# Two edits on TensorE's list: first block-attention scores without the wait on the value tiles' evictions, the sparse gates' token layout behind the next projection

## The reference, cut to what matters

```python
# first block: block attention (moba), stick-breaking attention, latent attention
proj = hn @ w_in
qa, ka, va = ...                       # 8 heads of 64
y_a = moba_attention(partial_rope(qa), partial_rope(ka), va)
# second block: sparse attention with three branches, a gate for each head and branch
proj = h @ w_in[l]
q_a, kv_a, g_a, q_b, k_b, v_b, uv_c = jnp.split(proj, IN_OFFSETS, axis=-1)
o_a = nsa_attention(..., jax.nn.sigmoid(g_a).reshape(B, S, NSA_HEADS, 3), ...)
kc = compress(k_cmp, ...)              # gelu(blocks @ w1) @ w2, the same for the values
out = gb[..., 0:1] * o_cmp + gb[..., 1:2] * o_slc + gb[..., 2:3] * o_win
```

## Time and profile before

| what | value |
|---|---|
| median of 3 runs | 2306.53 us (2305.97 to 2306.60) |
| the profiled execution, its own time | 2306.26 us |
| its span, first to last instruction | 2304.6 us |
| around the span | 1.7 us |
| PE busy | 2242.3 us, 97% |
| DVE, ACT, POOL busy | 71%, 54%, 3% |
| transfers | 467 MB, 203 GB/s on average |
| share of PE in the chain that ended last | 88% |

### The profile page before, as it was taken

One profiled execution on the slowest core, in us unless ns is written; L12 is line 12 of the kernel. 1 busy time (PEld: TensorE's weight loads), 2 busy tenths in 40 slices (PEclk: granted clock), 3 DMA queues, 4 the chain that ended last, 5 costly groups with the idle time before them and its releaser, 6 DMA issues.

```text
span 2304.6 us, 38375 instructions
## 1 busy us (share of the span) xinstructions
PE 2242.3 (97%) x14760; PEld 2007.8 (87%) x14760; DVE 1632.8 (71%) x2331; ACT 1234.9 (54%) x1729; POOL 75.0 (3%) x143
## 2 busy tenths in 40 slices
PE   3999999999999999999999999999999999999999
PEld 2888999988888888999988889899888898898888
DVE  7888777678778887677685667666756676667655
ACT  4444567564446446585554465656544555565443
POOL 0100000000000100000000000000000000000000
PEclk9999999999999999999999999999999999999999
DMA  8887465547666875655555546334555463344552
GB/s 321 298 290 270 166 226 178 199 159 282 253 239 218 284 282 187 221 189 215 192 202 198 182 160 207 147 128 166 195 186 183 150 240 140 137 165 176 190 187 104
DMA packets 79509, 467.32 MB, mean 203 GB/s; under 512 B 10080, under 2 KB 10800, under 8 KB 33168
## 3 DMA queue, kind: packets, MB, share of 16 engines
q1 hardware_dynamic: 58480, 389.12, 47.2%
q0 software_dynamic: 19312, 71.74, 8.8%
q10 hardware_dynamic: 1584, 4.62, 0.5%
HBM read 458.56 MB, written 1.05 MB: 199 GB/s over the span
## 4 chain that ended last, share of the span: by engine, by line
PE 88%; ACT 4%; DVE 4%; issue 1%; DMA 1%; ACTq 1%; DVEq 1%
PE ps L811 21%; PE ps L526 17%; PE ps L528 16%; PE ps L527 16%; PE ps L813 10%; DVE wlo L1716 2%; PE ps L640 2%; DMA adat<-in_ada 1%; PE ps L654 1%; PE ps L687 1%; ACT merged L1270 1%; DVE hx L1820 1%; ACT whi L1156 1%; PE ps L606 0%; PE ps L596 0%
## 5 line engine op out<-in xcount | busy, mean ns | idle before, releaser
L1716 DVE TENSOR_TENSOR wlo<-raw,whi 128x2048 fp32r<-128x2048 f32 x360 | 823.7, 2291 | 208.9 <-ACT whi L1156 195.2
L1156 ACT ACTIVATE whi<-raw 128x2048 fp32r<-128x2048 f32 x359 | 686.2, 1913 | 223.5 <-PE ps L528 219.4
L811 PE MATMUL ps<-hx,whi 128*128 128x512 f32 x2112 | 749.8, 399 | 5.3 <-DVE hx L1820 3.7
L813 PE MATMUL ps<-hx,wlo 128*128 128x256 f32 x2112 | 593.4, 281 | 0.0
L811 PEld LDWEIGHTS ps<-hx,whi 128*128 128x128 f32 x2112 | 397.7, 188 | 105.2 <-issue 4.7
L526 PE MATMUL ps<-hx,whi 128*128 128x256 f32 (+1 forms) x1424 | 410.8, 288 | 1.1 <-DVE wlo L1716 1.1
L527 PE MATMUL ps<-hx,whi 128*128 128x256 f32 (+1 forms) x1424 | 402.6, 283 | 0.0
L528 PE MATMUL ps<-hx,wlo 128*128 128x256 f32 (+1 forms) x1424 | 402.6, 283 | 0.0
L813 PEld LDWEIGHTS ps<-hx,wlo 128*128 128x128 f32 x2112 | 399.7, 189 | 2.1
L526 PEld LDWEIGHTS ps<-hx,whi 128*128 128x128 f32 (+1 forms) x1424 | 272.1, 191 | 7.8 <-issue 4.8
L527 PEld LDWEIGHTS ps<-hx,whi 128*128 128x128 f32 (+1 forms) x1424 | 272.4, 191 | 0.2
(11 more groups left out here) (276 smaller groups left out, 2944.5 us busy)
## 6 DMA issues: line engine op xcount, KB each, us to landing
raw<-in_w SPq DMA_DIRECT2D x360, 1024.0 KB, 4.9
adat<-in_ada POOLq DMA_DIRECT2D x128, 512.0 KB, 4.7
raw<-in_ada SPq DMA_DIRECT2D x4, 512.0 KB, 8.3
blk<-in_block POOLq DMA_DIRECT2D x2, 926.5 KB, 5.4
set_a<-set_b SPq DMA_DIRECT2D x24, 64.0 KB
x<-in_x POOLq DMA_DIRECT2D x1, 1024.0 KB, 10.2
raw<-in_ada ACTq DMA_DIRECT2D x2, 512.0 KB, 14.3
set_b<-in_ada SPq DMA_DIRECT2D x2, 512.0 KB, 12.6
```

The costliest lines, as they stand in the source:

```text
L811: mm(ps[:, bank + i, :].rearrange("p (a s) -> p a s", a=2), whi[:, slot, col:col + P], hx[:, :, k, :], start=(k == 0), stop=False)
L813: last = mm(ps[:, bank + i, 0:S], wlo[:, slot, col:col + P], hhi[:, k, :], start=False, stop=(k == KD - 1))
L1156: A(whi[:, slot, :], raw[:, slot, :], ACT.Copy).then_inc(*T.counts("hi_ready"))
L1716: tt(wlo[:, slot, :], raw[:, slot, :], whi[:, slot, :].bitcast(F32), ALU.subtract)\
```

## The change

Two edits on PE's list; the lists of the other engines stay as they are, except that all line numbers behind the first edit are lower by one. The first takes away a wait for the last eviction (the second value tile) ahead of the first scores, and leaves the wait for the ropes. The second moves the two transposes of the gates behind the 48 matmuls of tile 6. The wait for the gates' eviction (`pj_out`), which stood ahead of the transposes, stays where it was, now ahead of tile 6.

```diff
                     project("tokens")
                     project("tokens")
-                    pe.wait_ge(*T.nth("pj_out", T.n["fills"]))
                     wait_ropes(4)
...
                     pe.wait_ge(*T.nth("pj_out", T.n["fills"]))

                     def gates_by_token():
                         for t in range(2):
                             last = mm(ps[:, 6, t * 32:t * 32 + 24], gT[0:24, t * P:(t + 1) * P],
                                       c("ident", 24)[:, 0:24], start=True, stop=True)
                         return last

+                    project("features")
                     aux(gates_by_token)
-                    project("features")
                     for kind in range(2):
                         pe.wait_ge(*T.next("xb_ready"))
```

## The result

The changed kernel takes 2311.62 us (median of 13 executions, 2310.79 to 2313.11) against 2306.53: 5.1 us more, a ratio of 1.0023 with a 95% interval of 1.0015 to 1.0031. The interval is clear of 1, so the kernel is slower. Of the 13 executions of the kernel before, one took 5648.3 us, for which nothing here gives a reason; the other 12 lie between 2305.27 and 2306.99.

What follows compares the result with a forecast made beforehand. The prediction took PE's own list plus its waits as the bound (PE busy 97% of the span). From 2306.53 us, -1.5 for the first edit and +6.7 for the second gave 2311.6 us, range 2308.5 to 2314.8.

Steps and rivals of the forecast that it cites:

- The sum: Whole kernel: -1.5 us from the first edit and +6.7 from the second, +5.2 in all, said as 2311.6 us.
- First edit: First scores in each of two layers: starting 0.21 us behind the projection's last matmul, 0.76 earlier, 1.5 us saved in all.
- Second edit, PE alone: PE at the gates' transposes: worth nothing, the 0.46 us wait stays, now ahead of tile 6.
- Second edit, ACT: ACT's in-order list: the gates' copy starts at 1402.69 instead of 1396.76, and the split of tile 8 waits with it.
- The stalls: PE waits for late `wlo` at tile 8 (1.6 us) and tile 9 (1.4 us); 3.3 us a layer, 6.7 in two.
- The margin: Tile 8's weights, ready at 1402.38 and now wanted at 1405.51, may be 3.1 us later; the copy moves by 5.9.
- free: Rival, chance 0.06: moved transposes cost nothing, tile 8's weights still come in time, only the first edit counts; 2305.0 us.
- No third stall: Tile 11: weights ready 1.5 us in time, so no further PE wait; the rival third stall, 2314.4 us, had chance 0.06.
- The clock: Rival, chance 0.07: PE's clock falls behind the stalls, 2.1 us lost once in each layer; 2315.8 us.
- only one stall: Rival, chance 0.05: DVE's split of tile 9 comes in time, so a layer costs 1.9 us; 2308.8 us.
- the first edit gives nothing: Rival, chance 0.03: another wait takes over at the first scores or the gain is lost later; 2313.1 us.

Runs made afterwards that it cites:

- E1: First edit alone on the kernel before: no wait for the last value tile's eviction ahead of the first scores; 2304.65 us against 2306.10.
- E4: Changed kernel with ACT's gates copy behind the split of tile 8 and PE's wait for the gates' eviction directly ahead of the transposes; 2303.77 us against 2306.10 before.
- E6: Changed kernel with only PE's wait for the gates' eviction moved from ahead of tile 6 to directly ahead of the transposes; 2310.26 us against 2306.66 before.
- E7: Changed kernel with the gates' transposes in the middle of tile 6, behind 24 of its 48 matmuls; 2305.83 us against 2306.37 before.
- E5: Changed kernel with DVE's second key rope behind the splits of tiles 9 and 10, first differential-attention rope two splits later; 2308.70 us against 2306.66 before.
- E3: Changed kernel with ACT's copy of the transposed gates moved behind the split of tile 8 and tile 6's eviction; 2305.11 us against 2306.10 before.

## Why the prediction was right, point by point

**The sum.** Forecast 2311.6, measured 2311.62 and 2311.45. The terms were -1.5 and +6.7; alone they measured -1.45 and +7.13. That the medians agree to 0.02 is luck: the 13 executions spread over 2.3 us, and 2311.6 was chosen between 2311.4 and 2311.7. What the traces bear out is each term to 0.1 us a layer. The prediction gave 0.67 to a slowdown beyond its bound of 2311.1; the median lies 0.5 above it, but the interval of the ratio reaches to both sides of it, so this part stays undecided.

**First edit.** Right in place and size. The scores stand 0.21 us behind the projection, the ropes' wait did not take over, E1 has the 1.5 us, and between the two layers' scores the traces have the 0.76 (E1 above: 0.8).

**Second edit, PE alone.** Right: the 0.46 us in front of L995 came back in front of tile 6, 0.9 in both layers as before. E4 and E6 show what the wait costs once it is moved as well: 1.3 to 1.5 us, where I had 1.2.

**Second edit, ACT.** Right: from tile 6's start at 1395.91 the copy came after 6.60, forecast 6.58 (1402.69 - 1396.11).

**The stalls.** Right. I counted them from start to start, 1.6 and 1.4. The rows say 1.40 and 1.31, since they count from the modelled end of the last matmul, 0.28 behind its start where the next could have followed after 0.12. From start to start the first is 1406.90 - (1402.40 + 0.10 + 2.82) = 1.58, the second 1411.35 - (1406.90 + 0.10 + 2.88) = 1.47. The second is 0.1 above the forecast: PE began 0.15 behind the split's end (1411.20), not 0.05, as in E7 (0.15 again). Tile 11 came 21.86 us behind tile 6's start (1417.77 - 1395.91), where it had been 18.47 behind L995's (1414.58 - 1396.11): 3.39 for the first layer against 3.33 forecast. The second layer has 1893.88 - 1872.04 = 21.84 against 1887.29 - 1868.82 = 18.47, 3.37.

**The margin.** Right in what followed from it, wrong in what it compared. The rival of the free transposes sets tile 8's 3.1 us against the 5.9 by which the copy moves. But `wlo` of tile 8 moves by less, by its own times 1404.74 - 1400.09 = 4.65, measured 4.67 from tile 6's start: that is 1.6 over the 3.1, the first stall. And the tile that runs late first is tile 9, at a hold-up of some 2.8 us (E7). Both tiles were over their limits, so the conclusion stands.

**No third stall.** Right. The split of tile 11 on ACT waited 1.23 us for its load, which landed 1411.68 - 1406.85 = 4.8 us after `wlo` of tile 8 was done; `wlo` was ready at 1413.63 + 2.29 = 1415.92, 1.8 us in time.

**The clock.** It did not fall. The matmuls behind the stalls keep their pace of 0.12: from tile 9 at 1411.35 to tile 11 at 1417.77 are 6.42 us with the first matmul's 0.1, against 6.37. The granted clock agrees. In the stretch of the stalls (columns: PE, PEld, DVE, ACT, POOL busy, then granted clock, DMA share, GB/s):

```profile
1401.00:1415.00 14.00, 11.29 (x91) 10.74 (x90) 10.05 (x7) 9.68 (x8) 0.00 (x0) 1.00 0.43 163
```

PE was busy for 11.29 of 14 us, and the clock stayed at 1.00, the level of 2.4 GHz. Alone this column would be weak evidence, and so is the earlier trace rows in the prediction. Early in the kernel, where the matmuls of 128x512 follow at 0.64 in both profiles, it reads 0.50 after the change and 1.00 before it:

```profile
44.00:48.00 4.00, 4.00 (x13) 3.42 (x14) 3.40 (x10) 4.00 (x9) 0.15 (x1) 0.50 0.99 414
44.00:48.00 4.00, 4.00 (x13) 3.42 (x14) 3.41 (x10) 4.00 (x9) 0.20 (x1) 1.00 0.99 417
```

So the column can miss a slow stretch, and the pace decides. The Trainium skill (TensorE: Matmul & The Clock Gate, Part 1: The HAM clock gate) says that the clock falls once PE has been idle for long enough. The trace doesn't contradict it: two stalls of 1.40 and 1.31 us with tile 8's matmuls between them brought no fall.

The other rivals: *free* fell by the four new waits, *only one stall* by the second of them in each layer, *the first edit gives nothing* by E1, and E5 shows what one stall comes to: 2308.7, for which the prediction had 2308.8.

## What to carry to other kernels

When an instruction is moved on one engine, look at the list of the engine that waits for it: what is queued behind that waiting instruction moves too. Here a copy of 0.21 us took the next weight tile's conversion along, and 5.95 us of delay cost 3.4 us a layer, of which 3.05 are stalls; half the delay cost 0.28 of stalls; and with the copy moved as well there were none. Follow the delay through to each later tile: the slack of the first tile (here 4.4 us) says nothing of the next one's (2.8). And a wait has to move with the instructions that need it, or the edit frees nothing.

## What was not expected

The slow first matmuls last differently long from one execution to the next. Before, the pace of 0.64 us ends between 47.89 and 48.50; in the profile after, with the same instructions on PE up to there, it lasted 1.3 us longer (start us, us):

```profile
49.12 0.63 PE L811 MATMUL ps<-hx,whi 128*128 128x512 f32 x1
49.76 0.47 PE L811 MATMUL ps<-hx,whi 128*128 128x512 f32 x1
50.19 0.40 PE L811 MATMUL ps<-hx,whi 128*128 128x512 f32 x1
```

This is time at 1.2 GHz ahead of the rise: the granted clock there reads 0.50 (the rows above). At 0.64 against 0.35 from one such matmul to the next, 1.3 us more of it lose 1.3 x (1 - 0.35 / 0.64) = 0.6 us. The first scores came at 275.78 where the prediction has 274.98, 0.8 late, before the second edit had any part; the 0.6 is most of that. It is not the only thing that varies there. In the nine profiles without the first wait the first scores start between 275.01 (E5) and 275.78, and E3, where the slow pace ends early (its last slow matmul starts at 47.06), has 275.76. What else moves them stays open. The 0.8 us are a third of the spread between executions of one kernel, and a reason to compare single profiles over short stretches only.
